# Sums of squares added one tile later in half-width projections, and closed by one product instead of two

## The reference, cut to what matters

```
def rms_norm(x, g):
    xf = x.astype(jnp.float32)
    y = xf * lax.rsqrt(jnp.mean(xf * xf, axis=-1, keepdims=True) + EPS)
    return (y * g.astype(jnp.float32)).astype(x.dtype)
...
    x = x + merged @ w_out                      # a residual projection
    a, g = jnp.split(rms_norm(x, norm_ffn_g) @ w_ffn_in, 2, axis=-1)
    return x + (jax.nn.silu(a) * g) @ w_ffn_out # another one
```

## Time and profile before

| | before |
|---|---|
| median of 3 runs | 3034.93 us |
| profiled execution | 3031.36 us |
| its span | 3029.6 us |
| PE busy | 2962.4 us (98%) |
| PE loading weights | 2379.6 us (79%) |
| POOL busy | 2168.2 us (72%) |
| DVE busy | 1330.6 us (44%) |
| ACT busy | 682.6 us (23%) |
| TensorE clock granted, mean | 0.996 |

### The profile page before, as it was taken

How to read it: one execution, slowest core, us unless ns; L and a number is a source line. 1 busy time by engine, 2 the same in 40 slices (tenths; PEclk the granted TensorE clock), 3 DMA queues, 4 the chain that set the end, 5 groups by cost and what they waited for, 6 DMA issues and landing times.

```text
span 3029.6 us, 43192 instructions
## 1 busy us (share of the span) xinstructions
PE 2962.4 (98%) x13980; PEld 2379.6 (79%) x13980; DVE 1330.6 (44%) x2190; ACT 682.6 (23%) x1366; POOL 2168.2 (72%) x3010
## 2 busy tenths in 40 slices
PE   9999999999999999999999999999999999999998
PEld 7768888888877688788887777788887777788886
DVE  6753243122565533443345765422236775431223
ACT  5321111010234211210102543310012333310101
POOL 8557777787965577787888655587777446777875
PEclk9999999999999999999999999999999999999999
DMA  5222223222332122322224322122222112222222
GB/s 188 68 71 91 98 92 112 97 97 97 108 121 71 67 95 96 113 96 95 97 97 137 110 75 67 56 98 97 97 98 98 63 63 84 91 91 97 97 97 90
DMA packets 80902, 285.78 MB, mean 94 GB/s; under 512 B 8720, under 2 KB 9616, under 8 KB 79472
## 3 DMA queue, kind: packets, MB, share of 16 engines
q1 hardware_dynamic: 76432, 266.65, 26.3%
q10 hardware_dynamic: 4320, 17.11, 1.6%
HBM read 279.20 MB, written 4.33 MB: 94 GB/s over the span
## 4 chain that ended last, share of the span: by engine, by line
PE 87%; DVE 8%; ACT 3%; issue 1%; POOL 0%; DVEq 0%; DMA 0%; ACTq 0%; SPq 0%; POOLq 0%
PE pa L722 40%; PE pd L722 38%; PE pd L1011 2%; PE po L1052 1%; ACT work L192 1%; PE pa L777 1%; PE pa L1023 1%; DVE t L204 1%; DVE work L200 1%; DVE h_lo L204 1%; DVE x_res L196 1%; DVE po L196 1%; ACT h_hi L192 1%; PE pd L1074 1%; DVE pair L204 1%
## 5 line engine op out<-in xcount | busy, mean ns | idle before, releaser
L668 POOL TENSOR_TENSOR w_lo<-w_raw,w_hi 128x256 fp32r<-128x256 f32 x2004 | 1539.6, 800 | 41.8
L663 POOL TENSOR_SCALAR w_hi<-w_raw 128x512 fp32r<-128x512 f32 x1002 | 630.4, 648 | 792.4 <-PE pa L722 443.7
L722 PE MATMUL pa<-h_hi,w_hi 128*128 128x512 f32 (+1 forms) x1912 | 755.3, 395 | 8.1 <-DVE t L204 4.4
L722 PE MATMUL pa<-h_hi,w_lo 128*128 128x512 f32 (+1 forms) x1912 | 742.9, 389 | 0.0
L722 PE MATMUL pa<-h_lo,w_hi 128*128 128x512 f32 (+1 forms) x1912 | 742.8, 388 | 0.0
L722 PEld LDWEIGHTS pa<-h_hi,w_hi 128*128 128x128 f32 x1912 | 360.3, 188 | 110.0 <-issue 28.8
L722 PEld LDWEIGHTS pa<-h_hi,w_lo 128*128 128x128 f32 x1912 | 360.1, 188 | 75.1
L722 PEld LDWEIGHTS pa<-h_lo,w_hi 128*128 128x128 f32 x1912 | 360.5, 189 | 73.3 <-issue 1.9
L722 PE MATMUL pd<-b_hi,w_hi 128*128 128x512 f32 x992 | 390.6, 394 | 13.4 <-DVE x_res L196 7.8
L722 PE MATMUL pd<-b_hi,w_lo 128*128 128x512 f32 x992 | 386.4, 390 | 0.0
L722 PE MATMUL pd<-b_lo,w_hi 128*128 128x512 f32 x992 | 386.3, 389 | 0.0
(11 more groups left out here) (218 smaller groups left out, 3107.6 us busy)
## 6 DMA issues: line engine op xcount, KB each, us to landing
w_raw<-in_w SPq DMA_DIRECT2D x501, 512.0 KB, 3.2
mrg<-in_nabias ACTq DMA_DIRECT2D x2, 2048.0 KB, 11.0
x_res<-in_x SPq DMA_DIRECT2D x8, 256.0 KB, 5.7
mrg<-in_mem ACTq DMA_DIRECT2D x2, 1024.0 KB, 4.8
kept_mem<-m_hi ACTq DMA_DIRECT2D x2, 1024.0 KB, 5.3
out_y<-mrg ACTq DMA_DIRECT2D x8, 256.0 KB, 2.1
mrg<-in_mem SPq DMA_DIRECT2D x1, 1024.0 KB, 8.7
vbuf<-in_count ACTq DMA_DIRECT2D x2, 512.0 KB, 3.4
```

What stands on the lines that cost most here:

```text
L663: ins = nc.gpsimd.tensor_scalar(w_hi[:, j, half], raw[:, j % RR, half], 1.0, 1.0, ALU.mult, ALU.mult)
L668: ins = nc.gpsimd.tensor_tensor(w_lo[:, j, part], raw[:, j % RR, part], w_hi[:, j, part].bitcast(F32), ALU.subtract)
L722: ins = mm(out, a, b, start=(first and k == 0 and e == 0), stop=(last and k == k_n - 1 and e == 2))
```

## The change

Three edits, in the program of PE and in that of DVE. ACT, POOL and SP keep their instructions and their order.

1. In all norms but the final one DVE adds the square of tile 7 too, and this addition is now the one that writes `acc`. It is one more addition for each of ten norms.
2. In those ten norms PE sums `acc` alone, with one product; it waits for the last addition. The final norm keeps two products.
3. In the three half-width residual projections DVE's order is changed: the square of tile m - 1 is added between the addition of tile m to x and the remainder of tile m. The last square is added at the end.

```diff
@@ stream_norm of PE
                 def sum_up():
+                    if not final:
+                        pe.wait_ge(acc_part, summed)
+                        mm(bank[:, :], ones, acc, start=True, stop=True).then_inc(acc_used, 1)
+                        return
                     pe.wait_ge(acc_part, summed - 1)
                     mm(bank[:, :], ones, acc, start=True, stop=False)
                     pe.wait_ge(sx_full, squared)
@@ DVE
-            def prepare(m, name=None, split=True):
+            def prepare(m, name=None, split=True, final=False):
 
                 if split:
                     remainder(m, name)
-                i = n.take("acc_part")
-                if m == KT - 1:
+                add_square(m, final)
+
+            def add_square(m, final=False):
+
+                i, end = n.take("acc_part"), KT - 2 if final else KT - 1
+                if m > end:
                     return v.give(acc_part)
                 dve.wait_ge(sx_full, n.at("sx_full", i))
-                if m == KT - 2 and n.n.get("acc_used"):
+                if m == end and n.n.get("acc_used"):
                     dve.wait_ge(acc_used, n.last("acc_used"))
-                v.tensor_tensor(acc if m == KT - 2 else po[0][:, :], po[0][:, :], pair2[:, i % 2], ALU.add)\
+                v.tensor_tensor(acc if m == end else po[0][:, :], po[0][:, :], pair2[:, i % 2], ALU.add)\
                     .then_inc(acc_part, 1)
...
                     for m in range(KT):
                         add_x(m)
-                        prepare(m, name, split)
+                        prepare(m, name, split, not split)
...
@@ half_residual of DVE
                     add_x(m, m % 2 == 1)
-                    prepare(m, name)
+                    if m:
+                        add_square(m - 1)
+                    remainder(m, name)
+                add_square(KT - 1)
```

## The result

The changed kernel takes 3014.54 us (median of 4 runs, 3013.83 to 3020.44). The kernel before takes 3035.24 us in the same measurement (4 runs, 3034.58 to 3039.91). The ratio is 0.9933 with an interval of 0.9921 to 0.9944, so the change takes off 20.7 us (17 to 24). Forecast were 3015.4 us and 19.5 us less. The ratio is not the quotient of the two medians, so the difference that it gives can be off from that of the medians by about a microsecond. Where a difference in us follows a ratio here, both are given.

The account below looks back on a forecast made before the run. PE was taken to bound the kernel, but DVE's turn the half-width stretches. Sums 8.1 us plus stretches 11.4 make 19.5 us off 3034.93, so 3015.4 us, range 3010 to 3023 (8 in 10).

Parts of the forecast that it names:

- The sums, 7.7 us for nine: At the sums of nine norms, PE keeps all of the dropped product's time, 0.86 us each.
- The rival in which PE waits for DVE's last addition: At the sums, waiting replaces the second product and nothing is gained there: 3023.5 us, chance 0.04.
- The first norm, 0.4 us between bounds of 0 and 0.86: First norm's sum: the dropped product's gain may be swallowed by a later PE wait for POOL's weights; 0.4 us taken.
- the transfer behind the earlier trace: First norm: POOL had waited 5.53 us for a transfer; if it comes no earlier, the 0.86 us are swallowed.
- The half-width stretches, 3.8 us each: Third tile to sum in three half-width projections: the new DVE order gains 3.8 us each, 11.4 in all.
- DVE's new turn, 1.77 us + remainder: DVE's time per half-width tile as the sum of its parts, 2.75 us with the mean remainder, against PE's 2.73.
- a remainder of 0.98 us: DVE's remainder in the half-width stretches, taken at the mean over the program, near 0.98 us.
- DVE would then wait for PE ahead of its addition to x: Expected sign in the half-width stretches: DVE idle before its addition to x instead of before the remainder.
- The rival of the shared port: Half-width stretches: remainders meet POOL's instructions each time, take 1.26 us, DVE stays the bound: 3020.8 us, chance 0.16.
- The extra addition costs 0 elsewhere: DVE's added square in ten norms delays nothing that matters: cost 0, without cover at most 0.8 us, once.
- The sum, 19.5 us: Whole program: 8.1 us from the sums plus 11.4 us from the half-width stretches.
- The inner range of the terms: Whole program: the terms were said to give 3014.4 to 3016.5 us, within the forecast's own 3012 to 3019.

Follow-up runs that it names:

- the product done twice: Changed kernel with the one product of each of the ten norms done twice, the second writing over the first: 3026.19 us.
- The order alone: Kernel before with only DVE's new order in the half-width projections, two products kept in every norm: 3024.35 us, ratio 0.9962.
- the two useless additions: One overwritten DVE addition per half-width tile: before the remainder in the kernel before, 3041.09 us; behind the remainder in the changed kernel, 3033.64 us.
- the useless addition outside the gap: Changed kernel with one useless DVE addition behind the remainder in each tile of the half-width projections: 3033.64 us, ratio 0.9993.
- the three measurements: The changed kernel timed three times against the kernel before: 3014.54, 3019.53 and 3018.69 us.
- the second measurement's profile: Profile of the changed kernel, without further edit, from its second timing: 3019.53 us, ratio 0.9949.

## Why the prediction was right

*The sums, 7.7 us for nine.* Right: eight times 0.85 and once 0.73 us, 7.5 us. That they are PE's work and not a wait was shown by the product done twice. The rival in which PE waits for DVE's last addition took place at one norm only, the first, where the sum takes 1.84 instead of 1.32 us; the addition ends at 21.76 + 0.69 = 22.45 us there, where I had worked out 22.1. At 1933 us the addition ends at 1932.60 + 0.69 = 1933.29, 0.06 us ahead of the product, and the sum takes 0.13 us longer than the others:

```profile
1932.60 0.69 DVE L196 TENSOR_TENSOR qs<-po,pair 128x512 f32<-128x512 f32 x1
```

```profile
1933.35 1.13 PE L847 MATMUL pa<-qs,mats 128*128 128x512 f32 x2
```

*The first norm, 0.4 us between bounds of 0 and 0.86.* It gave 0.1 us by the starts, and nothing on the average of the traces. The doubt was right and its reason was not. Not the transfer behind the earlier trace rows takes the gain back, but DVE's list: PE waits for the extra addition, and 7 us later for `pair`, which stands behind it and behind eight remainders of the memory.

*The half-width stretches, 3.8 us each.* They gave 3.84, 3.75 and 3.87 us. The order alone gave 11.5 us in the time by its ratio (10.4 by the medians). The mechanism was a quarter of DVE's turn spent waiting, and the two useless additions showed it from both sides: 5.8 us inside the gap, 14.1 us outside it.

*DVE's new turn, 1.77 us + remainder.* It is about 1.87 us + remainder, because the addition of the square waits 0.23 and not 0.13 us behind the addition to x. Against that the remainders were hardly slower in the denser stretches. Their mean over the three is 0.86 us, and it was 0.85 before (the 0.84 of the prediction is a median):

```profile
L204 DVE SCALAR_TENSOR_TENSOR h_lo<-x_res,par,h_hi x8: 751/754/999, 1843.9 to 1863.2; 128x512 fp32r<-128x512 f32 x8
```

I had taken a remainder of 0.98 us. Over the eight tiles the turn is 2.72, 2.78 and 2.70 us in the three stretches, and PE needs 2.73 us for a tile. The prediction said that DVE would then wait for PE ahead of its addition to x, and this did not come: DVE's idle time there is 0.13 us a tile, which is the hop from the instruction before it. Apart from 0.2 us at most in a stretch, neither engine waits for the other. PE sets the length of the stretch, and DVE is level with it, which is why the useless addition outside the gap cost its whole length.

*The rival of the shared port.* It was not DVE that paid. POOL's groups in the first stretch, before and after:

```profile
L668 POOL TENSOR_TENSOR w_lo<-w_raw,w_hi 128x256 fp32r<-128x256 f32 x16 | 12.5, 812 | 0.3
L663 POOL TENSOR_SCALAR w_hi<-w_raw 128x512 fp32r<-128x512 f32 x8 | 4.8, 623 | 20.4 <-PE pd L722 20.4
```

```profile
L668 POOL TENSOR_TENSOR w_lo<-w_raw,w_hi 128x256 fp32r<-128x256 f32 x16 | 13.6, 883 | 0.3
L663 POOL TENSOR_SCALAR w_hi<-w_raw 128x512 fp32r<-128x512 f32 x8 | 6.2, 799 | 15.5 <-PE pd L722 15.5
```

POOL's instructions grew from 812 to 883 and from 623 to 799 ns, and POOL had idle time for it. The timelines of both engines in all three stretches say more. POOL has 72 instructions there. Before, 12 of them begin while a remainder is running on DVE, and these take 1.04 to 1.06 us; the other 60 take at most 0.75. After, 24 begin so, and take 1.05 to 1.26 us; the other 48 take at most 0.75. There is no exception. The remainders that begin within the first 0.26 us of a POOL instruction are 12 of 24 before and 12 of 24 after, and these alone take 0.90 us or more; the others take at most 0.77. So the denser order doubled the meetings in which POOL comes second and left those in which DVE does as they were. The Trainium skill, "SBUF — State Buffer", section "Who interferes with whom", says that of two such instructions the one that comes second waits. The trace agrees at each meeting in these stretches. The one that comes second grows by what is left of the first, less a constant: a POOL instruction by 0.31 to 0.54 us with 0.45 to 0.69 us of the remainder left (0.14 less each time), a remainder by 0.15 to 0.30 us with 0.37 to 0.49 us of POOL's usual time left (0.2 less). Had the new meetings fallen the other way round, the stretch would have kept some of its loss. At 1650 and 2600 us it was DVE's instructions that grew, which was not in the sum: 1.4 us.

*The extra addition costs 0 elsewhere.* Right in nine norms: PE loses at most 0.13 us on `qs`, and for the remainders of the memory in the two norms of the earlier trace rows, which come later now, it waits no longer than before. Wrong at the first norm, where remainders of the memory stand behind the addition too. The prediction counted only two such norms, and at the third the addition cost what the product gave.

*The sum, 19.5 us.* The places give 17.7 us. What was too high is the missing deduction of 1.4 us and the first norm's 0.3; the three measurements (20.7, 15.2, 17.9 us) lie around both. That the first median fell 0.9 us from the forecast is partly luck. The same kernel measured 3019.5 and 3018.7 us later, 3 to 4 us above the forecast, and at the few places where the clock falls single executions differ by more than that. The inner range of the terms, 3014.4 to 3016.5 us, does not follow from the bounds given either: both upper bounds together, 20.3 us, give 3014.6.

## What to carry over

Where an engine's turn sets the pace, look for waits inside the turn, and put into them work of the tile before whose input has long been ready; the order gave 10 to 12 us with no instruction less. The same order is worth nothing where that engine waits for another once per tile. An instruction added to the engine that seems idle is free only where nothing that others wait for stands behind it in that engine's list; at the first norm something did. And after a shift in time, look again for instructions far behind the change that meet a busy neighbour at another moment: they gave back 1.4 of 19 us here.

## What the runs showed of the hardware

TensorE's granted clock falls to half (1.2 of 2.4 GHz) for 3.4 us, and at some places for 6.8 or 10.2, in some executions and not in others. In the changed kernel's profile one such stretch stands at 1598 us, directly behind PE's 1.97 us of idle time:

```profile
1597.33 0.49 PE L722 MATMUL pd<-b_hi,w_hi 128*128 128x512 f32 x1 [1.97 <-DVE x_res L196]
...
1599.12 0.63 PE L722 MATMUL pd<-b_hi,w_lo 128*128 128x512 f32 x1
```

```profile
1598.00:1601.20 3.20, 3.20 (x9) 2.48 (x8) 2.19 (x3) 1.28 (x3) 3.12 (x5) 0.50 0.35 131
```

Matmuls there start 0.43 us apart instead of 0.227, and the place came out 1.6 us behind the second measurement's profile, where the clock was 1.00. Apart from the last microseconds of the program, such stretches are found in the twelve profiles near 95, 136, 860, 904, 940, 1600, 1730, 1910, 2320, 2620 and 2660 us, in another choice each time. Each of them begins during idle time of PE or less than 2 us behind it, and this idle time is 1.4 to 5.3 us long. The reverse does not hold: the same 1.97 us near 1600 us are followed by a lower clock in two of the three traces of the changed kernel. Between these places, from 1300 to 1590 us and from 1950 to 2300 us, all twelve traces keep the same pace to 0.03 us.

So the spread of some 10 us between runs of one kernel is made at few places. Two traces of the changed kernel, of 3013.83 and 3024.30 us, differ by 4.7 us between 90 and 215 us, by 1.5 us each near 860 and 1730 us, and by about 1 us each near 2320 and 2620 us; the three half-width stretches are equal to 0.02 us in them. The difference of two single traces can be off by several microseconds where that of a stretch is good to a few hundredths.
